# Expert weights laid out kind by kind, four experts' parts in one transfer, and a fourth ring region of whole places

## What is computed

```python
def hier_moe(hn, w_grp, w_exp, w_gate, w_up, w_down):
    ...                                   # two of 64 experts for each token, within one of 8 groups
    def expert_block(args):               # a block of tokens that share one expert
        xb, e = args
        hh = jax.nn.silu(xb @ w_gate[e]) * (xb @ w_up[e])     # 1024 -> 256
        return hh @ w_down[e]                                 # 256 -> 1024
```

## Time and profile before

| | us |
|---|---|
| median of 3 runs | 2373.58 (2372.71 to 2374.41) |
| the profiled execution | 2370.78 |
| its span | 2369.0 |
| TensorE busy | 2186.3 (92%) |
| VectorE busy | 1080.7 (46%) |
| ScalarE busy | 384.0 (16%) |
| SyncE's DMA queue, share of 16 engines | 67.4% |
| moved by DMA | 619.39 MB, 261 GB/s over the span |

### The profile page before, as it was taken

How to read it: one execution, slowest core, us unless ns; L and a number is a source line. 1 busy time by engine, 2 the same in 40 slices (tenths; PEclk the granted TensorE clock), 3 DMA queues, 4 the chain that set the end, 5 groups by cost and what they waited for, 6 DMA issues and landing times.

```text
span 2369.0 us, 27951 instructions
## 1 busy us (share of the span) xinstructions
PE 2186.3 (92%) x10672; PEld 1324.2 (56%) x10672; DVE 1080.7 (46%) x2074; ACT 384.0 (16%) x917; POOL 54.3 (2%) x95
## 2 busy tenths in 40 slices
PE   8999999999999999999999999888999998777776
PEld 7865558854885555884585544343437543333332
DVE  6665647665765665666322433233333343222222
ACT  2211331102210232110301210000003220000001
POOL 1200000000100000000000000000000000000000
PEclk9999999999999999999999999999999999898989
DMA  9542435532953334533592799999997289999998
GB/s 337 190 176 89 160 105 174 202 111 97 301 177 143 125 132 135 171 149 111 167 328 107 295 413 409 417 422 422 422 414 280 107 328 412 416 422 422 422 421 330
DMA packets 223561, 619.39 MB, mean 261 GB/s; under 512 B 16813, under 2 KB 122102, under 8 KB 179558
## 3 DMA queue, kind: packets, MB, share of 16 engines
q1 hardware_dynamic: 216400, 610.26, 67.4%
q0 software_dynamic: 1600, 5.06, 0.6%
q10 hardware_dynamic: 5462, 2.72, 0.4%
HBM read 616.94 MB, written 1.05 MB: 261 GB/s over the span
## 4 chain that ended last, share of the span: by engine, by line
PE 66%; DMA 19%; SPq 9%; DVE 2%; ACT 1%; issue 1%; DVEq 0%; POOL 0%; POOLq 0%; ACTq 0%
PE PS L2787 22%; DMA ring<-expert_parts 19%; PE PS L2870 11%; PE PS L1846 5%; SPq L1133 5%; PE PS L1739 4%; PE PS L2974 3%; PE PS L2928 3%; PE PS L3115 2%; SPq L1130 2%; SPq L1114 1%; PE PS L1799 1%; PE PS L865 1%; PE PS L1310 1%; PE PS L2957 1%
## 5 line engine op out<-in xcount | busy, mean ns | idle before, releaser
L1846 PE MATMUL PS<-ring,arena 128*32 128x512 f32 x1728 | 241.5, 692 | 117.7 <-DMA ring<-expert_parts 115.0
L2787 PE MATMUL PS<-ring,xT 128*128 128x256 f32 x1056 | 243.1, 379 | 3.5 <-ACT xT L2074 3.5
L2787 PEld LDWEIGHTS PS<-ring,xT 128*128 128x128 f32 x1056 | 200.2, 190 | 31.2 <-ACT xT L2074 4.2
L1799 PE MATMUL PS<-arena,xn 128*128 128x128 f32 x1280 | 203.2, 297 | 13.0 <-DVE h L1645 13.0
L1846 PEld LDWEIGHTS PS<-ring,arena 128*32 128x32 f32 x1728 | 64.1, 124 | 266.7 <-issue 239.1
L1799 PEld LDWEIGHTS PS<-arena,xn 128*128 128x128 f32 x1280 | 164.0, 189 | 73.1 <-issue 41.3
L2787 PE MATMUL PS<-arena,xn 128*128 128x256 f32 x704 | 165.7, 379 | 0.0
L1652 DVE TENSOR_TENSOR arena<-PS,small 128x512 f32<-128x512 f32 x62 | 42.8, 691 | 269.0 <-PE PS L1799 269.0
L2870 PE MATMUL PS<-ring,arena 128*128 128x512 f32 x352 | 162.8, 592 | 0.0
L2787 PEld LDWEIGHTS PS<-arena,xn 128*128 128x128 f32 x704 | 130.6, 190 | 16.1
L1815 PE MATMUL PS<-arena 128*128 128x512 f32 (+1 forms) x300 | 138.4, 603 | 0.0
(11 more groups left out here) (433 smaller groups left out, 2886.5 us busy)
## 6 DMA issues: line engine op xcount, KB each, us to landing
ring<-expert_parts SPq DMA_DIRECT2D x316, 1024.0 KB, 18.9
ring<-ffn_gate_up SPq DMA_DIRECT2D x88, 1024.0 KB, 10.4
ring<-ffn_down SPq DMA_DIRECT2D x44, 1024.0 KB, 7.3
arena<-expert_parts SPq DMA_DIRECT2D x73, 256.0 KB, 12.3
arena<-expert_parts SPq DMA_DIRECT2D x13, 1024.0 KB, 13.4
ring<-w_in SPq DMA_DIRECT2D x16, 768.0 KB, 6.0
ring<-conv_w_in SPq DMA_DIRECT2D x12, 1024.0 KB, 12.7
ring<-expert_parts SPq DMA_DIRECT2D x16, 512.0 KB, 15.2
```

The costliest lines, as they stand in the source:

```text
L1799: last = mm(PS[:, bank, at * P:(at + 1) * P], lhsT=xn[0:w, t, k * P:(k + 1) * P], rhs=onehot[0:w, t, :], start=t == 0, stop=t == nt - 1)
L1846: last = mm(PS[BLK * j:BLK * (j + 1), 2, :], lhsT=xgT[:, k, j * BLK:(j + 1) * BLK], rhs=w[k % HALF], start=k == 0, stop=k == KD - 1)
L2787: last = mm(out, lhsT=a[:, k, :], rhs=b[:, 256 * k:256 * (k + 1)], start=k == 0, stop=k == 3)
```

## The change

`expert_parts` is laid out as layer, kind, partition, expert. The parts of one kind for neighbouring experts now follow each other on a partition, 8 KB each, and the rows of one part lie 64 x 8 KB = 512 KB apart. The ring is laid out by kind as well, so that a quad is one stretch of 32 KB a partition, and one transfer of 4 MB (`128x8192`) fills it. Four places in one piece form `WHOLE`, a fourth region for quads (still four transfers of 1 MB). The places of pieces form `BITS` (quad 4) with fewer pieces, and are used once; so are `META_ROWS` and `ROUTING`, which hold one or two parts of quad 5. From quad 5 on the written groups (7 in layer 0, 3 in layer 1) go round `RING[0]`, `RING[1]`, `RING[2]`, `WHOLE`. Groups up to 13 are read by number in a hardware loop of one transfer for each quad; groups 14 and 15 come from the list as before, part by part. The weights of the attention move to other addresses of the ring.

```diff
-    return np.ascontiguousarray(np.concatenate([gu, dn], 2))
+    return np.ascontiguousarray(np.concatenate([gu, dn], 2).transpose(0, 2, 3, 1, 4))
...
-        CYCLE = [RING[0] + RING[1] + RING[2] + [MORE[0], AHEAD[3]] + SPARE[3 - i:] + SPARE[:2]
-                 + [AHEAD[1], AHEAD[2], MORE[1], AHEAD[0], ROUTING] for i in (0, 1)]
-        WRITTEN = (7, 5)
...
+        ringf = ring[:, :, :].rearrange("p s w -> p (s w)")
+
+        def ring_parts(n, j0, j1):
+
+            return ringf[:, (GROUP * n + j0) * PART:(GROUP * n + j1) * PART]
...
+        RING = [[Place(ring_parts(n, j, j + 1)) for j in range(GROUP)] for n in range(3)]
+        WHOLE = [Place(arena[:, 11712:11712 + PART]), Place(rowsf[:, 1024:1024 + PART]), Place(arena[:, 8896:8896 + PART]),
+                 Place(xT[:, :, :].rearrange("p k t -> p (k t)")[:, 0:PART])]
+        BITS = [Place(const[:, LEVELS_AT:LEVELS_AT + 1024], sgw[:, :, :].rearrange("p g t -> p (g t)"), arena[:, 10944:11456]),
+                Place(mixed_rows[:, 0:1024], const[:, LEVELS_AT - 512:LEVELS_AT], rowsf[:, 3072:3584]),
+                Place(rowsf[:, 3584:4096], arena[:, 0:512], arena[:, 5424:5936], arena[:, 6192:6704]),
+                Place(arena[:, 13760:15296], arena[:, 15552:16064])]
+        META_ROWS = Place(h[:, 2, :], xn[:, 2, :])
+        ROUTING = Place(arena[:, 576:576 + PART])
+        ALONE = [[ROUTING], [META_ROWS, ROUTING]]
+        WRITTEN = (7, 3)
+        STATIC = NE // GROUP - 2
+
+        def quad(i, g, n):
+
+            q = 3 * g + n
+            if g >= WRITTEN[i] or q < 3:
+                return RING[n]
+            if q < 5:
+                return (WHOLE, BITS)[q - 3]
+            return (RING + [WHOLE])[(q - 5) % 4]
 
         def home(i, g, n, j):
 
-            if g < WRITTEN[i]:
-                return CYCLE[i][(UNITS * g + GROUP * n + j) % len(CYCLE[i])]
-            return RING[n][j]
-
-        def in_one_piece(space):
-
-            return any(space is v for kind in RING for v in kind) or any(space is v for v in AHEAD[:3] + MORE[:1])
+            if (g, n) == (1, 2) and j < len(ALONE[i]):
+                return ALONE[i][j]
+            return quad(i, g, n)[j]
 
         def signal_of(i, g, n):
 
...
-        def first_load(sp, i, space, qs=None):
...
-            else:
-                for q in range(4) if qs is None else qs:
-                    sp.dma_start(space[q], src[:, 512 * q:512 * (q + 1)]).then_inc(landed, 16)
+        def parts_of(i, n, e, count):
+
+            return A["expert_parts"][i, n][:, bass.ds(e, count), :].rearrange("p e w -> p (e w)")
+
+        def ring_load(sp, i, g, n, j0=0, j1=GROUP):
+
+            loaded = signal_of(i, g, n)
+            place = RING.index(quad(i, g, n))
+            return sp.dma_start(ring_parts(place, j0, j1), parts_of(i, n, g * GROUP + j0, j1 - j0)).then_inc(loaded, 16)
+
+        def place_load(sp, i, g, n, j, xs=None):
+
+            place = home(i, g, n, j)
+            src, loaded = parts_of(i, n, g * GROUP + j, 1), signal_of(i, g, n)
+            for x in range(len(place.pieces)) if xs is None else xs:
+                at, v = place.first(x), place.pieces[x]
+                sp.dma_start(v, src[:, at:at + v.shape[1]]).then_inc(loaded, 16)
 
         def mla_weights(sp, groups):
 
...
+                place_load(sp, 0, 1, 1, 3, (0,))
+                place_load(sp, 0, 1, 1, 0, (0, 1))
+                place_load(sp, 0, 1, 1, 1, (0, 1))
+                sp.wait_ge(slot_free[0], 1)
+                ring_load(sp, 0, 0, 0, 0, 3)
+                sp.wait_ge(slot_free[1], 1)
+                ring_load(sp, 0, 0, 0, 3, 4)
+                ring_load(sp, 0, 0, 1, 0, 2)
+                sp.wait_ge(slot_free[2], 1)
+                ring_load(sp, 0, 0, 1, 2, 4)
+                ring_load(sp, 0, 0, 2, 0, 1)
+                sp.wait_ge(slot_free[3], 1)
+                ring_load(sp, 0, 0, 2, 1, 4)
+                sp.wait_ge(S.pe_step, 1)
+                place_load(sp, 0, 1, 0, 1)
+                place_load(sp, 0, 1, 0, 2)
+                place_load(sp, 0, 1, 1, 0, (2,))
...
+
                 if n < 2:
                     sp.wait_ge(gu_used[i][n], GROUP * (g + 1))
                 else:
                     sp.wait_ge(M[i].dn_used, 2 * GROUP * (g + 1))
 
-            size = len(CYCLE[i])
-            for at in range(size, UNITS * WRITTEN[i]):
-                if at == size or (at - size) % GROUP == 0:
-                    part_used(at - size)
-                g, n, j = at // UNITS, at % UNITS // GROUP, at % GROUP
-                whole(g, n, j, signal_of(i, g, n))
-                if at == size + GROUP - 1:
+            for q in range(5, 3 * WRITTEN[i] + 3):
+                g, n = q // 3, q % 3
+                before = max(p for p in range(q) if quad(i, p // 3, p % 3) is quad(i, g, n))
+                part_used(before // 3, before % 3)
+                if q == 5:
+                    ring_load(sp, i, 1, 2, len(ALONE[i]), GROUP)
                     sp.wait_ge(S.routed, i + 1)
-                    first_load(sp, i, ROUTING)
-            for n in range(3):
-                for j in range(GROUP):
-                    last = max(at for at in range(UNITS * WRITTEN[i]) if at % size == GROUP * n + j)
-                    if j == 0 or last % GROUP == 0:
-                        part_used(last)
-                    e = WRITTEN[i] * GROUP + j
+                    place_load(sp, i, 1, 2, len(ALONE[i]) - 1)
+                elif quad(i, g, n) is WHOLE:
+                    for j in range(GROUP):
+                        place_load(sp, i, g, n, j)
+                else:
+                    ring_load(sp, i, g, n)
+            with sp.Fori(WRITTEN[i] + 1, STATIC) as g:
+                for n, loaded in enumerate((gu_loaded[i][0], gu_loaded[i][1], M[i].dn_loaded)):
                     if n < 2:
-                        gate_up(slice(e, e + 1), j, n)
+                        sp.wait_ge(gu_used[i][n], g * GROUP)
                     else:
-                        down(slice(e, e + 1), j)
...
-            def arrived(g, n, static):
+            def arrived(g, n, static, listed):
 
                 if static is not None:
                     pe.wait_ge(signal_of(i, static, n), LANDED[i, static, n])
                     return
-                pe.wait_ge((gu_loaded[i][0], gu_loaded[i][1], M[i].dn_loaded)[n], g * 64 + max(SURPLUS[i][n], 0))
-
-            def gate_up(g, half, static=None):
+                loaded = (gu_loaded[i][0], gu_loaded[i][1], M[i].dn_loaded)[n]
+                if listed:
+                    pe.wait_ge(loaded, g * 64)
+                else:
+                    pe.wait_ge(loaded, g * 16 + max(SURPLUS[i][n], 0))
...
+            with pe.Fori(WRITTEN[i], STATIC) as g:
+                group(g, False)
+            for n in range(3):
+                pe.sem_inc((gu_loaded[i][0], gu_loaded[i][1], M[i].dn_loaded)[n], (64 - 16) * (STATIC - 1) - max(SURPLUS[i][n], 0))
             pe.wait_ge(S.routed, i + 1)
             groups = pe.value_load(ng[0:1, 0:1], min_val=NE // GROUP, max_val=MAX_GROUPS)
             final = pe.value_load(ng_last[0:1, 0:1], min_val=NE // GROUP - 1, max_val=MAX_GROUPS - 1)
-            with pe.Fori(WRITTEN[i], final) as g:
-                group(g)
+            with pe.Fori(STATIC, final) as g:
+                group(g, True)
```

More of the change, by code:

```diff
@@ L587, in chunks_of @@
             return [v[:, 512 * q:512 * q + 512] for q in range(v.shape[1] // 512)]
-        RING = [[chunks_of(ring[:, j, PART * n:PART * (n + 1)]) for j in range(GROUP)] for n in range(3)]
-        AHEAD = [chunks_of(xT[:, :, :].rearrange("p k t -> p (k t)")[:, 0:PART]), chunks_of(rowsf[:, 1024:1024 + PART]),
-                 chunks_of(arena[:, 8896:8896 + PART]),
-                 chunks_of(const[:, LEVELS_AT:LEVELS_AT + 1024]) + [sgw[:, :, :].rearrange("p g t -> p (g t)"), arena[:, 10944:11456]]]
@@ new lines, in build, with __init__, first @@
+        class Place:
+            def __init__(self, *pieces):
+                self.pieces = pieces
+                self.chunks = [c for v in pieces for c in chunks_of(v)]
+                assert len(self.chunks) == PART // 512
+            def first(self, x):
+                return 512 * sum(len(chunks_of(v)) for v in self.pieces[:x])
+        RING = [[Place(ring_parts(n, j, j + 1)) for j in range(GROUP)] for n in range(3)]
+        WHOLE = [Place(arena[:, 11712:11712 + PART]), Place(rowsf[:, 1024:1024 + PART]), Place(arena[:, 8896:8896 + PART]),
+                 Place(xT[:, :, :].rearrange("p k t -> p (k t)")[:, 0:PART])]
@@ L619, in signal_of, with loads_of @@
             return (gu_loaded[i][0], gu_loaded[i][1], M[i].dn_loaded)[n]
+        def loads_of(i, g, n):
+            if g == 0:
+                return 2
+            if (g, n) == (1, 2):
+                return 1 + sum(len(v.pieces) for v in ALONE[i])
+            v = quad(i, g, n)
+            return 1 if v in RING else sum(len(u.pieces) for u in v)
         def landed_tables():
@@ L629, in landed_tables @@
```

(4 more changed lines are left out.)

182 lines of the change are left out of this document (72 added, 110 removed).

## The result

The changed kernel takes **2352.14 us** (median of 4 runs, 2349.66 to 2354.97), the kernel before beside it 2373.14 (2371.25 to 2374.41): a ratio of 0.9917, 95% interval 0.9904 to 0.993, so 0.8% faster. The forecast was 2356; the measured time stands at the lower edge of the range. The profiled execution took 2352.11 us, span 2350.3, against 2370.78 and 2369.0 before: 18.7 us less, where the sum of the prediction gave 17.7.

A forecast was written before the change was run, and what follows sets the result against it. The expert transfers were taken to bind both layers' loops. Savings of 14.9 and 4.8 us less 2.0 of pauses gave 17.7 us, so 2353.1 profiled and, with the median 2.8 us above, 2356 us; range 2352 to 2384.

The forecast's parts named there:

- What bounds: In both expert loops the transfers bind, at 422 GB/s, 869 us in all from first ring release to last landing.
- The price of a row: Each row a DMA engine moves costs a fixed 9.1 ns whatever its length; a 32 KB row takes 1215.1 ns.
- Parts 1 to 3 together: Expert loops: rows of 32 KB save 14.9 us, fewer pieces save 4.8, fewer places lose 2.0; sum 17.7 us.
- The pauses: Stream waits for places at layer 0's quads 9 and 10 (0.2 and 1.2 us), layer 1's quad 6 (0.6 us).
- The term of 2.2 us: Start of a load that finds an idle queue: 4.7 us from issue to landing, less 2.5 of its own.
- Rival C: Stock of loaded parts too small: 5 or 6 MB of places missing once in each layer, 2383 us; chance 0.04.
- The end of a layer, SyncE, TensorE: 0: Groups 14 and 15 keep their short rows; SyncE's issues and TensorE's register steps lie under queue and waits: 0.
- The size: Whole kernel: median of 2356 us, 0.7% less; chance of the forecast 0.58.
- Rival A: Expert transfers: rows 512 KB apart slow the stream by 3.5%, 2383 us; chance 0.19, with 1 to 2.5% 0.08.
- Rival B: Long rows bring nothing, as engines cut them or the constant belongs to each 8 KB: 2371 us; chance 0.11.

## Why the prediction was right, point by point

- *What bounds.* Right. The full windows moved from 421 and 422 GB/s to between 429 and 433, and the time went with them.
- *The price of a row.* Right, and the extrapolation held to the nanosecond: 1215 ns for 32 KB, 29.14 us a group against 29.2. The three lengths within one design give 9.2 to 9.6 ns a row for 9.1. The estimate of 3.5 ns, which the prediction worked out from the Trainium skill ("DMA: Bandwidth & Descriptors", "Why small descriptors are slow (HBM only)"), would have ended at 2368 us. The eight runs of the changed kernel lie between 2349.7 and 2355.0, so the measurement decides.
- *Parts 1 to 3 together.* Right. Layer 0: 7.15 + 13 x 0.219 - 1.4 = 8.6 us forecast, 8.9 and 8.3 measured in the two executions. Layer 1: 7.67 + 9 x 0.219 - 0.6 = 9.0 forecast, 7.9 and 10.0 measured. The split is borne out by the kernel with 8 KB rows. Against it the long rows bring 13.3 and 14.8 us in the two stretches together (14.6 forecast for these quads) and 13.4 by the medians; what is left against the kernel before is 3.5 us by stretches (2.8 forecast). The 2.8 were not taken apart further: no run changes the pieces alone.
- *The pauses.* At their places, and too long in the forecast by half a microsecond to one in layer 0. The term of 2.2 us from a release to a full stream is larger than what a gap costs: in the trace of after the first packet starts 1.0 us after the issue at 1327.90, and the sixteenth 1.7 us after it. The term was read from issue to landing, which also holds what comes behind the last byte. The cover under them was thin: with one region less the engines stand still for microseconds at a time, and 31 us are lost. Rival C was not wrong in its mechanism, only in the number of regions from which it decides; its 2383 us is the time of the three-region kernel, though by luck in part: rival C counted 27 us of missing places at the old cost of a row, and the run shows 34 us of pauses.
- *The end of a layer, SyncE, TensorE: 0.* Right as a sum. What the prediction did not see is that in layer 0 the last group turns from waiting for transfers to being bound by TensorE. So a further gain in the transfers of that last group would bring nothing; one ahead of 1715.68 us, where the chain of after still has a transfer, would be passed on.
- *The size.* 2356 against 2352.1. The ratio's interval is a gain of 16.6 to 22.8 us; the 17.7 of the sum lie in it, so what is left between the two numbers is not told from noise. By stretches the change's share is 16.8 us in one profiled execution and 18.3 in the other, on both sides of the 17.7. The rest of the difference between the profiled executions lies ahead of the first release, in the attention and at the end, where executions of one kernel differ by as much. That the median came out 4 us better than 2356 is shown by no mechanism here.
- *Rival A* had 0.27 of the chance. Its mechanism exists: at eight times the distance of this layout it costs 32% of the changed kernel's time, at four times 4% and at twice 0.4%, of which the traces put only about half where the transfers bind. At 512 KB it costs nothing here. The chance was too high only in hindsight: no row of before could have told.
- *Rival B* is refuted by the two shorter rows, and by one transfer of short rows.

## What to carry to other kernels

Where the DMA engines are full, count the rows that they move: here each cost a fixed 9 ns or so, from 2 KB to 32 KB and however many shared a transfer. So lay out memory so that what is fetched together is one long row in each partition. Before that, walk through the places by hand and see that the buffers which go round still cover the time from a release to the next use; one region of four was worth more here than all the long rows. And when the new layout sets rows a large power of two apart, try a padding of 4 KB: at 4 MB it took nearly all of the loss away, at 512 KB there was none. The loss begins with the short rows.

## What was not expected of the hardware

- Rows exactly 4 MB apart take the read rate from 430 GB/s to between 114 and 339 with engines that are full to 0.97 or more. Rows 2 MB apart slow rows of 8 KB (420 ns for 316 in the mean) and not rows of 32 KB (1223 ns for 1224). At 1 MB rows of 2 KB already take 105 ns for 88. 4 KB of padding at 4 MB gives 316 and 1223 ns again, and 88 and 102 ns for the rows of 2 KB in the two layers' last quads.
- One execution can have half the clock in its last microseconds (0.50 in three windows of 2 us) and another of the same kernel the full one; from the last packet to the end it is 15.0 and 13.5 us, while the medians agree within 0.7 us.
